# Sums of squares, modulation rows and weight halves at the start of a two-block transformer kernel

## What is computed

```python
mx = (jax.nn.silu(c) @ ada_w[layer] + ada_b[layer]).reshape(b, 1, N_MOD, D_MODEL)
mc = (jax.nn.silu(c_ctx) @ ada_w[layer] + ada_b[layer]).reshape(N_MOD, D_MODEL)
hx = modulate(rmsnorm(x, norm1_g[layer]), mx[:, :, 0], mx[:, :, 1])
hc = modulate(rmsnorm(ctx, norm1_g[layer]), mc[0], mc[1])
ux = hx @ w_in[layer]
uc = hc @ w_in[layer]
```

## Time and profile before

| | us |
|---|---|
| median of 3 runs | 860.38 (857.07 to 861.55) |
| profiled execution, its own time | 855.95 |
| its span, first to last instruction | 853.9 |
| TensorE busy | 838.1 (98%) |
| VectorE busy | 584.3 (68%) |
| ScalarE busy | 476.2 (56%) |
| GpSimd busy | 408.7 (48%) |
| mean granted TensorE clock, share of full | 0.995 |

### The profile page before, as it was taken

How to read it: one execution, slowest core, us unless ns; L and a number is a source line. 1 busy time by engine, 2 the same in 40 slices (tenths; PEclk the granted TensorE clock), 3 DMA queues, 4 the chain that set the end, 5 groups by cost and what they waited for, 6 DMA issues and landing times.

```text
span 853.9 us, 14859 instructions
## 1 busy us (share of the span) xinstructions
PE 838.1 (98%) x5870; PEld 769.6 (90%) x5870; DVE 584.3 (68%) x1192; ACT 476.2 (56%) x793; POOL 408.7 (48%) x193
## 2 busy tenths in 40 slices
PE   9799999999999999999999999999999999999997
PEld 5478899999799999999999988999999888888886
DVE  2769989976767797676767869776548444454445
ACT  6444334443656665555555765555446766666665
POOL 0037612223653478888888400200000688888883
PEclk8999999999999999999999999999999999999999
DMA  9786656654476556556555546264535556666661
GB/s 354 277 315 211 232 222 198 208 191 161 156 240 208 168 168 199 184 176 192 177 193 174 166 146 198 86 201 134 183 114 172 174 173 189 184 197 187 198 184 71
DMA packets 44743, 161.38 MB, mean 189 GB/s; under 512 B 5105, under 2 KB 5377, under 8 KB 43522
## 3 DMA queue, kind: packets, MB, share of 16 engines
q1 hardware_dynamic: 44384, 159.38, 57.1%
q10 hardware_dynamic: 290, 1.05, 0.3%
HBM read 159.37 MB, written 1.05 MB: 188 GB/s over the span
## 4 chain that ended last, share of the span: by engine, by line
PE 79%; DVE 11%; ACT 4%; POOL 2%; issue 2%; DMA 2%; ACTq 0%; DVEq 0%; SPq 0%; POOLq 0%
PE bank L665 11%; PE bank L670 11%; PE bank L668 11%; PE bank L1099 9%; PE bank L1105 5%; PE bank L1188 2%; PE bank L1190 2%; PE bank L1192 2%; PE bank L1138 2%; PE bank L1136 2%; PE bank L1140 2%; DVE wlo L527 2%; POOL wlo L527 2%; PE bank L998 2%; DVE ada_kT L1845 2%
## 5 line engine op out<-in xcount | busy, mean ns | idle before, releaser
L527 POOL TENSOR_TENSOR wlo<-raw,whi 128x1024 fp32r<-128x1024 f32 (+1 forms) x167 | 388.4, 2345 | 418.2 <-ACT whi L1370 418.0
L1370 ACT ACTIVATE whi<-raw 128x1024 fp32r<-128x1024 f32 (+1 forms) x253 | 258.5, 1026 | 65.2 <-PE bank L670 22.6
L1818 DVE SCALAR_TENSOR_TENSOR accs<-bank,vec,accs 128x189 f32<-128x189 f32 (+4 forms) x440 | 161.3, 435 | 71.2 <-ACT accs L1681 71.2
L665 PE MATMUL bank<-h,whi 128*128 128x256 f32 x504 | 143.7, 286 | 0.0
L670 PE MATMUL bank<-h,whi 128*128 128x256 f32 x504 | 142.3, 283 | 0.0
L668 PE MATMUL bank<-h,wlo 128*128 128x256 f32 x496 | 140.5, 283 | 0.7 <-DVE wlo L527 0.7
L527 DVE TENSOR_TENSOR wlo<-raw,whi 128x1024 fp32r<-128x1024 f32 x86 | 105.1, 1236 | 17.8 <-ACT whi L1370 17.1
L665 PEld LDWEIGHTS bank<-h,whi 128*128 128x128 f32 x504 | 96.7, 192 | 0.7 <-issue 0.3
L670 PEld LDWEIGHTS bank<-h,whi 128*128 128x128 f32 x504 | 96.7, 192 | 0.0
L668 PEld LDWEIGHTS bank<-h,wlo 128*128 128x128 f32 x496 | 95.2, 192 | 1.1 <-DVE wlo L527 1.0
L1099 PE MATMUL bank<-h,whi 128*128 128x512 f32 x352 | 88.4, 392 | 0.5 <-DVE gl L1815 0.4
(11 more groups left out here) (359 smaller groups left out, 1884.7 us busy)
## 6 DMA issues: line engine op xcount, KB each, us to landing
raw<-in_up SPq DMA_DIRECT2D x88, 512.0 KB, 3.5
raw<-in_w_in SPq DMA_DIRECT2D x45, 512.0 KB, 4.5
raw<-in_down SPq DMA_DIRECT2D x44, 512.0 KB, 3.6
ada_kT<-in_adaT SPq DMA_DIRECT2D x22, 512.0 KB, 4.0
ada_sc<-in_ada SPq DMA_DIRECT2D x8, 1024.0 KB, 19.1
raw<-in_w_out SPq DMA_DIRECT2D x16, 512.0 KB, 4.4
raw<-in_w_in_t SPq DMA_DIRECT2D x12, 512.0 KB, 4.8
ada_vM<-in_adaT SPq DMA_DIRECT2D x10, 512.0 KB, 4.5
```

What stands on the lines that cost most here:

```text
L527: return e.tensor_tensor(wlo[:, j % HL, 0:k], raw[:, j % RAW, 0:k], whi[:, j % HL, 0:k].bitcast(F32), ALU.subtract)
L665: e.matmul(ps, wh[:, k, :], xh(k), start=k == 0, stop=False)
L1370: e.activation(whi[:, j % HL, 0:(k1 - k0) * 128], raw[:, j % RAW, 0:(k1 - k0) * 128], ACT.Copy).then_inc(S.hi.up(j))
L1818: return e.scalar_tensor_tensor(out=out, in0=a, scalar=s, in1=b, op0=o1, op1=o2)
```

## The change

- **Squares in two sums.** DVE adds the 8 squares in six additions to two sums (squares 0 to 3, 4 to 7). TensorE adds these two over the partitions, 8 products in place of 16.
- **Idle products.** Three more of 512 columns before the first sum, one of 512 in place of two of 256 between the sums, two in place of one after `turn_rows(0)`, one more after `mod_rows(1)` and one after `step(0, (0, 1))`; those from `turn_rows(0)` on go to bank 3.
- **Rows 16 to 23** land in the halves of modulation blocks 2 to 5 once TensorE is done with block 5 (two of them once it is done with block 7), between the loads of chunks 4 to 7. The ring of three buffers serves rows 24 to 47. ACT's copy of the values waits until row 23 is used, since it overwrites them.
- **Low halves** of chunks 4 to 15 are DVE's, and not POOL's. On DVE they are put into the loop over FF0 to FF7 (chunk j+4 behind `kk` of j) and behind the scan.
- **Order on DVE.** Low halves 0 to 3 and the scaled blocks of x (`normed_x`) are interleaved otherwise with the operand; two rows come into the operand's loop, at k = 5 and 6; FF5, FF6 and FF7 have two rows each; fewer rows are left behind the scan.
- FF4's low products stand at its end (`late`).

The diff, without one hunk in which `mod_rows` waits for the block's first event:

```diff
--- before.py
+++ after.py
@@ -52,7 +52,8 @@
 AHEAD = ("down", "w_out2", "wo")
 FTILES = [(f, t) for f in range(2) for t in range(2 * NFF)]
 FPAIRS = [(f, i) for f in range(2) for i in range(NFF)]
-ADA_OF = [list(range(16 + j, 48, 3)) for j in range(3)]
+EARLY = list(range(16, 24))
+ADA_OF = [list(range(24 + j, 48, 3)) for j in range(3)]
 TOGETHER = 4
 NVEC1 = VOFF["ffn_conv_b"]
@@ -157,10 +158,8 @@
             out.append("pool")
         elif (name, n) == ("w_in2", 16):
             out.append("pool")
-        elif j < TOGETHER:
+        elif j <= ch("w_in", IN_Q + 3):
             out.append("dve")
-        elif j <= ch("w_in", IN_Q + 3):
-            out.append("pool")
         elif j <= ch(*LAST_IN):
             out.append("pool" if j % 3 == 0 else "dve")
         elif name in ("w_a", "w_b") or (name == "w_out" and n == 0):
@@ -369,7 +368,7 @@
             vec, conv, ident, msk, dft, mem = (landed(n) for n in ("vec", "conv", "ident", "msk", "dft", "mem"))
             poolw, gkw, invc = (landed(n) for n in ("poolw", "gkw", "invc"))
             crow = landed("crow")
-            sc = [landed(f"sc{k}") for k in range(KT)]
+            sc = [landed(f"sc{k}", ("block", "row")) for k in range(KT)]
             x = [landed(f"x{i}") for i in range(2)]
             ctx = [landed(f"ctx{i}") for i in range(2)]
             ada_in = [landed(f"ada{s}", ADA_OF[s]) for s in range(3)]
@@ -442,7 +441,7 @@
             modk = signal("modk", range(KT))
             xr = signal("xr", range(KT))
             ab1 = signal("ab1")
-            ssx = signal("ssx", range(4))
+            ssx = signal("ssx", ("01", "23", "half0", "45", "67", "half1"))
             both = signal("both")
             inv = signal("inv", NORMS)
             mod = signal("mod", ("amul2",))
@@ -588,8 +587,11 @@
         def ada_at(j):
-            s = (j - 16) % 3
-            return s, M["ada_kT"][:, s, :] if s < 2 else M["ada_vM"][:, :]
+            if j in EARLY:
+                i = j - EARLY[0]
+                return S.sc[i], "row", M["ada_sc"][:, 2 + i // 2, 4 * (i % 2):4 * (i % 2) + 4, :].rearrange("p a b -> p (a b)")
+            s = (j - 24) % 3
+            return S.ada_in[s], j, M["ada_kT"][:, s, :] if s < 2 else M["ada_vM"][:, :]
         def ht_bank(k):
             return M["ht"][:, k % 2, :]
@@ -808,10 +810,10 @@
                 return of("h2h", "h2l", S.xh, lambda k: (name, k), S.xl, lambda k: (name, k))
-            def keep_busy(n, width=512):
+            def keep_busy(n, width=512, bank=banks[7]):
                 for _ in range(n):
-                    e.matmul(banks[7][:, 0:width], M["sq"][:, 0, 0:128], M["sq"][:, 0, 0:width], start=True, stop=True)
+                    e.matmul(bank[:, 0:width], M["sq"][:, 0, 0:128], M["sq"][:, 0, 0:width], start=True, stop=True)
             w.wait_ge(S.idle, 0)
             keep_busy(3)
@@ -876,22 +878,26 @@
             keep_busy(1)
             slot, _ = aux_ring.take("x", S.xr, KT - 1)
             w.wait_ge(S.const, "ones")
-            for i in range(4):
-                w.wait_ge(S.ssx, i)
+            keep_busy(3)
+            for i in range(2):
+                w.wait_ge(S.ssx, f"half{i}")
                 for m in range(4):
-                    t = e.matmul(banks[6][:, m:m + 1], M["sqs"][:, 2 * i, m * 128:m * 128 + 128], ones[:, 0:1],
-                                 start=i == 0 and m == 0, stop=i == 3, skip_group_check=True)
-                if i < 2:
-                    keep_busy(1, 256)
+                    t = e.matmul(banks[6][:, m:m + 1], M["sqs"][:, 4 * i, m * 128:m * 128 + 128], ones[:, 0:1],
+                                 start=i == 0 and m == 0, stop=i == 1, skip_group_check=True)
+                if i == 0:
+                    keep_busy(1)
             t.then_inc(S.total.up("x"))
             w.wait_ge(S.rowc, "cs")
             mod_rows(0)
             w.wait_ge(S.ident, 0)
             spread("x", aux_bank("x"))
             turn_rows(0)
-            keep_busy(1)
+            w.wait_ge(S.rowc, "cb")
+            keep_busy(2, bank=banks[3])
             mod_rows(1)
+            keep_busy(1, bank=banks[3])
             step(0, (0, 1), lambda: turn_rows(1))
+            keep_busy(1, bank=banks[3])
             step(0, (2,))
             step(1, (0, 1))
             mod_rows(2)
@@ -916,7 +922,7 @@
                 aux_ring.until[i] = (S.hcl, KT - 1)
             for j in range(TOGETHER, 8):
                 slot, free = lin_ring.take(("ff", j), S.sgf, j)
-                lin("w_in", IN_FF + j, banks[slot][:, :], hc_all, free)
+                lin("w_in", IN_FF + j, banks[slot][:, :], hc_all, free, late=j == TOGETHER)
             slots = [lin_ring.take(("V", m), S.V, m) for m in range(4)]
             lin_rows("w_in_t", range(4, 8), 7, [banks[s] for s, _ in slots], hc_all, [f for _, f in slots],
                      [("V", m) for m in range(3)])
@@ -1492,6 +1498,7 @@
                 e.activation(sq_at(("ff", j)), lin_bank(("ff", j))[:, :], ACT.Sigmoid).then_inc(S.sgf.up(j))
             for n in range(4, 8):
                 splits(ch("w_in_t", n) + HL)
+            w.wait_ge(S.ada, EARLY[-1])
             for m in range(4):
                 w.wait_ge(*((S.tokens, ("V", m)) if m < 3 else (S.chunk, ch("w_in_t", 7))))
                 e.activation(M["V"][:, m, :], lin_bank(("V", m))[:, :], ACT.Copy).then_inc(S.V.up(m))
@@ -1840,8 +1847,8 @@
                 j = next(steps)
                 w.wait_ge(S.rowc, "cb")
-                slot, buf = ada_at(j)
-                w.wait_ge(S.ada_in[slot], j)
+                signal, event, buf = ada_at(j)
+                w.wait_ge(signal, event)
                 e.tensor_tensor_reduce(buf, buf, cb[:, :], 1.0, col("ada_b", j), ALU.mult, ALU.add,
                                        mod[:, j, 0:1]).then_inc(S.ada.up(j))
@@ -1869,10 +1876,16 @@
             tt(lbs[:, 4:8], a0, lbs[:, 0:4], ALU.subtract)
             tt(lbs[:, 8:12], a1, lbs[:, 0:4], ALU.subtract).then_inc(S.lb.up("less"))
-            for i in range(4):
-                w.wait_ge(S.sqx, 2 * i + 1)
-                tt(M["sqs"][:, 2 * i, :], M["sqs"][:, 2 * i, :], M["sqs"][:, 2 * i + 1, :],
-                   ALU.add).then_inc(S.ssx.up(i))
+            def add(i, j, key):
+                tt(M["sqs"][:, i, :], M["sqs"][:, i, :], M["sqs"][:, j, :], ALU.add).then_inc(S.ssx.up(key))
+
+            for i in (0, 4):
+                w.wait_ge(S.sqx, i + 1)
+                add(i, i + 1, f"{i}{i + 1}")
+                w.wait_ge(S.sqx, i + 3)
+                add(i + 2, i + 3, f"{i + 2}{i + 3}")
+                w.wait_ge(S.ssx, f"{i + 2}{i + 3}")
+                add(i, i + 2, f"half{i // 4}")
             inverse("x")
             def modulation(k):
@@ -1908,21 +1921,26 @@
             scaled(0)
             normed_x(1)
             operand_low(0)
-            normed_x(2)
+            los(1)
             modulation(1)
             scaled(1)
+            operand_low(1)
+            normed_x(2)
+            los(3)
+            modulation(2)
+            scaled(2)
+            operand_low(2)
+            los(4)
             normed_x(3)
-            operand_low(1)
-            los(2)
-            for k in range(2, KT):
+            for k in range(3, KT):
                 modulation(k)
                 scaled(k)
                 operand_low(k)
-                if k == 2:
-                    los(4)
-                if k < 4:
-                    normed_x(2 * k)
-                    normed_x(2 * k + 1)
+                if k == 3:
+                    for i in range(4, KT):
+                        normed_x(i)
+                if k in (5, 6):
+                    ada_step()
             for _ in range(4):
                 ada_step()
@@ -1947,7 +1965,9 @@
                 w.wait_ge(S.fk, ("f", j))
                 e.tensor_scalar(kk[:, :, d, h, :], f[:, :, d, h, :], -1.0, 1.0, ALU.mult,
                                 ALU.add).then_inc(S.fk.up(("k", j)))
-                ada_step()
+                los(ch("w_in", IN_FF + j) + HL + 1)
+                for _ in range(2 if j > 4 else 1):
+                    ada_step()
             suf, one255 = M["suf"], cst[:, 1:2].broadcast_to((128, 255))
             e.memset(suf[:, 0, :, 255:256], 1.0)
             e.memset(suf[:, 1, :, 0:1], 1.0).then_inc(own())
@@ -1960,6 +1980,7 @@
             w.wait_ge(own_dve, own_dve.n)
             for d in range(2):
                 tt(kk[:, 1, d, :, :], kk[:, 1, d, :, :], suf[:, d, :, :], ALU.mult).then_inc(S.kc.up(d))
+            los(ch("w_in", IN_Q + 3) + 1)
             for _ in range(4):
                 ada_step()
             for h in range(4):
@@ -2498,11 +2515,11 @@
                     at[0] = j + 1
             def ada(j):
-                slot, buf = ada_at(j)
-                e.dma_start(buf, D["adaT"][j, :, :]).then_inc(S.ada_in[slot].up(j), 16)
+                signal, event, buf = ada_at(j)
+                e.dma_start(buf, D["adaT"][j, :, :]).then_inc(signal.up(event), 16)
```

(26 more changed lines are left out.)

2 lines of the change are left out of this document (1 added, 1 removed).

## The result

| | before | after |
|---|---|---|
| median, us | 859.65 (857.07 to 861.55, 6 runs) | 853.65 (853.00 to 855.94, 6 runs) |
| profiled execution: its time, its span | 855.95, 853.9 | 854.29, 852.4 |
| granted TensorE clock in it | 0.995 | 0.999 |

The ratio of after to before is 0.9935 (0.9914 to 0.9955). By the medians the change is **6.0 us faster**, by the ratio 5.6, where 1.2 were forecast and 855.9 was the range's lower end. The two profiled executions are only 1.7 us apart, near the 1.2 forecast between them (855.95 to 854.7). So most of the gain is in executions that the first profile did not show.

A forecast was written before the change was run, and what follows sets the result against it. TensorE's columns were taken to bound the kernel from 60 us on, leaving gains mainly at the start. 0.9 us (start through loop) plus 0.3 behind gave 1.2 us: 859.2 us from the 860.4 median, range 855.9 to 862.3.

The forecast's parts named there:

- the clock's term: Start, 12.2 to 19.0 us: half clock costs 1.3 us in the sums and 0.9 in `mod_rows(0)`, 2.2 in all, on the path.
- with the same 1.2 off the median: Whole kernel: timed median, 4.4 us above the profiled execution, falls by the same 1.2 us, to 859.2 us.
- rival 1: Start: idle products also remove lost clock or pauses of the timed runs; half gives 857.0 us, all 854.8; chance 0.2.
- nothing shows the timed runs from inside: Argument against rival 1, which puts lost clock or pauses at the start of the timed runs.
- The mechanism of the start: Start: idle products hold full clock from 12 to 19 us; sums end at 14.4, `hch` of block 0 at 20.9.
- rival 2: From 8 to 19 us: idle products at half clock stand in the path, slower, 862.0 us; chance 0.17.
- The loop's 0.9 us: Operand's loop: last `hch` ends at 51.4 in place of 52.3; 0.9 us kept of 1.75 at block 0.
- Of the 0.2 idle from 116 to 130 and the short waits ... I take 0.3: Behind the feed forward groups: idle time and short waits for the scan's keys and values give 0.3 us.
- The list's waits for DVE's rows get fewer ... I take nothing for that: SP's transfer list: eight rows out of the ring mean fewer waits, which hold back transfers only; counted as nothing.
- The exchange of low halves: DVE takes 12 low halves, 14.9 us, and loses waits GpSimd caused, 6.2 us on `kk` alone: even or better.
- Rival 3: Behind the operand: DVE becomes the bound, FF5 to FF7 late, 862.2 us; over the value chunks too, 865; chance 0.13.
- Rival 4: Start and loop: rows at k = 5 and 6 take the start's whole gain, 860.4 us; chance 0.05.

The follow-up runs named there:

- no_idle: The changed kernel with its idle products put back as they were before; 855.38 us, 0.9960 of before.
- look1: The kernel before, unchanged, one single profiled execution; span 856.2 us.
- before_again: The kernel before, unchanged, run and profiled again; 857.52 us, 0.9984 of before.
- idle_only: The kernel before with only the new idle products, the two of 256 columns between the sums kept; 858.35 us, 0.9991 of before.
- sums_idle: The kernel before with the squares in two sums and the idle products; 856.87 us, 0.9975 of before.
- start_only: The kernel before with two sums, idle products and DVE's order of low halves and scaled blocks, rows and GpSimd's halves kept; 854.74 us, 0.9949 of before.
- better: The changed kernel with moved rows spread otherwise: one in the loop, two behind the first operand, two per group from the third; 852.06 us, 0.9921 of before.
- tail_out: The kernel before without the eight modulation rows behind the scan and their transfers, zeros in their place; 857.00 us, 0.9983 of before.
- start_tail: The kernel before with the edits of start_only and tail_out joined; 854.57 us, 0.9945 of before.
- start_low: The kernel before with start_only's edits, low halves 4 to 15 on VectorE and FF4's low products at its end; 856.74 us, 0.9977 of before.
- pool_low: The changed kernel with low halves 4 to 15 on GpSimd again; 859.85 us, 1.0001 of before.
- look3: start_only's kernel, one more single profiled execution; span 856.4 us.

## Why the prediction was wrong

- **The failing step is the clock's term, "2.2 in all", priced from one execution, and the 4.4 us between that execution and the median, kept as a constant: "with the same 1.2 off the median".** The one execution had 6.8 us at half clock at its start and a short span. An average execution of before has 13.6 us of low clock, one of the changed kernel 2.3 or 3.7. Some 10.6 us fewer at 0.23 us each (no_idle) to 0.34 (look1) are, by this estimate, 2.4 to 3.6 us of the mean span's 5.0 (857.0 to 852.0). The prediction had this as rival 1, at 0.2, and its far end was 854.8; the chip gave 853.65.
- **The gap between the profiled execution and the others is clock only in part.** In mean spans it is 3.1 us (853.9 to 857.0). The clock, 8.5 against 13.6 us, makes 1.2 to 1.7 of it. The pause behind `memT`, which came in three of the ten profiles that can have it and cost 2.3 us in before_again, is part of the rest; how much, and what else there is, stays open.
- **What stood against rival 1 was that "nothing shows the timed runs from inside".** But each timed run came with its time, and the profiled one was faster than all three. That is a reason to price its own luck, not to take its gap for a constant. That the two profiled executions lie 1.7 us apart, near the 1.2, does not bear out the sum: its terms were off both ways, as the points below show.
- **The mechanism of the start held, with one sign of rival 2.** Full clock from 12 to 19 us, and the sums' end, operands and FF4 within 0.7 us of the forecast, the idle products being 0.93 us each and not 0.8. What was missed is that the idle products do little alone: idle_only's clock fell all the same. The low clock is 9.9 us on average in idle_only, 7.1 in sums_idle, 5.7 in start_only. Why the order matters for the clock was not separated. The Trainium skill (TensorE: Matmul & The Clock Gate, Part 1) says that the moment of the change varies between runs. In the four profiles of before the clock fell at 12.2, 12.7, 10.1 and 11.5 us: the traces agree. The same place of the Trainium skill calls the loss at a start under 1% of a typical span and advises against fitting a count of slow products. It is under 1% here too, and was yet about half of this change's worth.
- **The loop's 0.9 us came out at 0.7**: the last operand 0.68 sooner (51.01 against 51.69), a wait of 0.91 before it, FF4 0.64 sooner. What the forecast took as given is that the two rows stand there: start_only, without them, begins FF4 2.35 us sooner. Of its lead of 1.7 on the changed kernel 0.7 stands at the first operand already (20.09 against 20.78), so the rows cost some 1.0 in the loop, where 0.7 was reckoned. better, with one row, begins FF4 0.8 us sooner than the changed kernel, and its span is 1.6 shorter: the waits before the last operand and at FF5 were on the path.
- **"Of the 0.2 idle from 116 to 130 and the short waits ... I take 0.3" was too little.** Between the two profiled executions ScalarE's third copy of a value starts 0.94 us sooner (101.22 and 100.28), its copy of the first score (`S`) 1.50 (123.66 and 122.16), and its copy of `kT` 1.75 (275.58 and 273.83): 0.8 us behind the forecast's 0.9. From there on nothing changes.
- **"The list's waits for DVE's rows get fewer ... I take nothing for that": the rows behind the scan were mis-sized at zero.** With them gone `memT` lands after 4.7 to 5.0 us, not 5.3 to 7.3, and none of the seven profiles without them has the pause. tail_out puts them at 1.5 us by the ratio, start_tail at nothing, and neither is clear of its interval; their price in the timed runs is not shown.
- **The exchange of low halves was even on the kernel of before, as argued** (0.9998), though not on top of the start's edits (start_low). Rival 3 did not come: TensorE waits 0.28 us for VectorE between 60 and 116. What the prediction did not have is that the rows without that exchange cost all the gain (pool_low).
- Rival 4 is excluded: FF4 starts 0.64 us sooner with two rows in the loop, and the ratio is 0.9935.

## What to carry to other kernels

A profiled execution that is faster than the timed ones is a sample, not the base: list the granted clock of every execution, take two or three more profiles of the unchanged kernel, and price a change at the start against the mean of them. Read from the trace where the low clock lies, since a stretch of it can cost nothing, as the one at 498 us in look1. Steps that hold the clock up have to be tried together: two idle products that took 1.88 us at full clock took 3.34 in the path once it had dropped anyway. When work is moved ahead onto an engine that is full, look at what another engine's work costs it there, and spread the moved pieces so that none stands before the last operand of a chain.

## What was not expected of the hardware

- One kernel on one core spent 6.8, 6.8, 10.2 and 13.6 us of its first 26 at half clock in four profiles; from profile to profile the operand moved by 0.48 us for each, the end of the kernel by only 0.34.
- 3.4 us at half clock at 498 us (look1) left the end of the kernel where it was; the same 3.4 us behind the pause at 222 (look3) went with a loss of 1.8.
- A pause of TensorE of 2.1 us at 222 us was followed by 3.4 us at half clock (look3), and the kernel came out 4.0 us later behind both, more than the pause's own length. In before_again a pause of 2.1 us was followed by no such stretch, and cost 2.3.
- A transfer of 1 MB landed after 4.7 to 5.0 us where no row was issued behind it (seven profiles), and where two of 512 KB each were (ten), after 5.3 to 5.7 in seven and 6.4 to 7.3 in three, with the rows issued as far behind it.
